# Two SwiGLU stages in seven block products each, with adaLN sums on VectorE, and x loaded first

## The reference

```python
def swiglu(h, w_gate, w_up, w_down):
    return (jax.nn.silu(h @ w_gate) * (h @ w_up)) @ w_down   # 1024 -> 2816 -> 1024
...
for l in range(DEPTH_2):                                     # two layers
    sh1, sc1, g1, sh2, sc2, g2 = jnp.split(c_act @ w_ada[l] + b_ada[l], N_MOD, axis=-1)
    ...
    x = layer_norm(DEEPNORM_ALPHA * x + g1[:, None, :] * y, ln1_g[l], ln1_b[l])
    h = modulate_2(x, sh2, sc2)
    y = swiglu(h, ffn_w_gate[l], ffn_w_up[l], ffn_w_down[l])
    x = layer_norm(DEEPNORM_ALPHA * x + g2[:, None, :] * y, ln2_g[l], ln2_b[l])
```

## Time and profile before

| | us |
|---|---|
| median of 3 runs | 1952.1 |
| lowest, highest | 1949.6, 1953.83 |
| profiled execution, its own time | 1950.68 |
| its span | 1948.9 |
| TensorE busy | 1888.5 |
| VectorE busy | 1291.9 |

### The profile page before, as it was taken

One profiled execution on the slowest core, in us unless ns is written; L12 is line 12 of the kernel. 1 busy time (PEld: TensorE's weight loads), 2 busy tenths in 40 slices (PEclk: granted clock), 3 DMA queues, 4 the chain that ended last, 5 costly groups with the idle time before them and its releaser, 6 DMA issues.

```text
span 1948.9 us, 23971 instructions
## 1 busy us (share of the span) xinstructions
PE 1888.5 (97%) x9600; PEld 1593.4 (82%) x9600; DVE 1291.9 (66%) x1969; ACT 814.6 (42%) x1238; POOL 466.0 (24%) x379
## 2 busy tenths in 40 slices
PE   4999999999999999999999999999999999999997
PEld 3788888887888887888788888877899778999996
DVE  6687655567667645665665555466677676777797
ACT  4677622352222235222522222248677553433333
POOL 4333210121111112001300000025643142445352
PEclk9999999999999999999999999999999999999998
DMA  9522366356565523542455442313211223323331
GB/s 334 153 85 66 113 222 238 120 193 238 211 221 201 188 87 117 186 151 93 168 201 187 173 151 87 108 65 130 71 58 52 87 72 101 109 95 101 108 100 52
DMA packets 134432, 267.65 MB, mean 137 GB/s; under 512 B 4576, under 2 KB 49648, under 8 KB 134321
## 3 DMA queue, kind: packets, MB, share of 16 engines
q1 hardware_dynamic: 129360, 248.59, 37.2%
q0 software_dynamic: 4960, 17.53, 2.5%
HBM read 261.84 MB, written 8.45 MB: 139 GB/s over the span
## 4 chain that ended last, share of the span: by engine, by line
PE 68%; DVE 3%; ACT 3%; POOL 2%; issue 1%; DVEq 0%; POOLq 0%; ACTq 0%
PE ps L720 22%; PE ps L722 21%; PE ps L721 21%; PE ps L880 1%; ACT t L1400 1%; ACT t L1396 1%; PE ps L869 1%; PE ps L858 0%; POOL t L2722 0%; PE ps L897 0%; PE ps L898 0%; PE ps L896 0%; DVE t L1889 0%; DVE t L1874 0%; POOL t L2531 0%
## 5 line engine op out<-in xcount | busy, mean ns | idle before, releaser
L720 PE MATMUL ps<-t 128*128 128x512 f32 (+1 forms) x2720 | 997.0, 367 | 12.1 <-POOL t L2626 5.2
L722 PE MATMUL ps<-t 128*128 128x512 f32 (+1 forms) x2720 | 989.6, 364 | 0.0
L721 PE MATMUL ps<-t 128*128 128x512 f32 (+1 forms) x2720 | 985.8, 362 | 0.0
L720 PEld LDWEIGHTS ps<-t 128*128 128x128 f32 x2720 | 513.2, 189 | 95.3 <-POOL t L2531 5.8
L722 PEld LDWEIGHTS ps<-t 128*128 128x128 f32 x2720 | 512.7, 189 | 84.6
L721 PEld LDWEIGHTS ps<-t 128*128 128x128 f32 x2720 | 513.1, 189 | 79.8 <-issue 1.0
L1810 DVE TENSOR_TENSOR t<-t 128x2048 fp32r<-128x2048 f32 x115 | 267.2, 2323 | 315.7 <-ACT t L1347 315.5
L1347 ACT ACTIVATE t<-t 128x2048 fp32r<-128x2048 f32 x115 | 219.7, 1911 | 465.2 <-PE ps L722 457.6
L1822 DVE CUSTOM_DVE_ANT_0 t<-t 128x1024 f32<-128x1024 f32 x144 | 174.8, 1255 | 6.8 <-DMA t<-in_adakv_t 3.6
L1874 DVE SCALAR_TENSOR_TENSOR t<-ps,t 128x512 f32<-128x512 f32 x184 | 131.7, 748 | 71.4 <-PE ps L722 68.1
L2531 POOL TENSOR_TENSOR t<-t 128x512 fp32r<-128x512 f32 x88 | 115.5, 1330 | 197.1 <-ACT t L1354 196.5
(11 more groups left out here) (196 smaller groups left out, 1894.7 us busy)
## 6 DMA issues: line engine op xcount, KB each, us to landing
t<-in_ada SPq DMA_DIRECT2D x48, 1024.0 KB, 5.9
t<-in_gate SPq DMA_DIRECT2D x22, 1024.0 KB, 5.2
t<-in_up SPq DMA_DIRECT2D x22, 1024.0 KB, 5.2
t<-in_down SPq DMA_DIRECT2D x22, 1024.0 KB, 5.1
t<-in_w_in SPq DMA_DIRECT2D x17, 1024.0 KB, 5.7
t<-in_w_mlp_in SPq DMA_DIRECT2D x16, 1024.0 KB, 5.3
t<-in_w_mlp_out SPq DMA_DIRECT2D x16, 1024.0 KB, 5.1
t<-in_ada_t POOLq DMA_DIRECT2D x13, 1024.0 KB, 6.2
```

The lines of the kernel that those rows point to most:

```text
L720: pe.matmul(o, wh, xh, start=first, stop=False)
L721: pe.matmul(o, wh, xl, start=False, stop=False)
L722: return pe.matmul(o, wl, xh, start=False, stop=last)
```

## The change

1. `plan_ffn2(l)` now plans both SwiGLU stages with S slots, in the order gate, up, gate, up instead of gate, gate, up, up (the last one had that), and `ffn2(l, ...)` is one function for both on each engine. The bank set of a slot is that of gate or up. One joined buffer each for gate and up remains (two before), and a spare one serves the second pair of weight sums (it was `csb[1]`, which the adaLN sums of the first SwiGLU read).
2. The 19 adaLN blocks of the first SwiGLU are spread over its slots 2 to 26 (counted from its first; 2, 3, 4, 6, 7, 8, 10, 11, 12, 14, 15, 16, 18, 19, 20, 22, 23, 24, 26), in two buffers instead of three. VectorE sums them at the end of the slot, behind the third join. SyncE loads each one slot ahead.
3. The second four shifts move from ahead of the joins of the first up slot of column group 5 to behind the third join of the last up slot; the column work `fox_cols` (before: `before()`, behind the residuals of the C slot) stands behind them in the first SwiGLU. Of group 5 the order is now gate, C slot of the down weights, up, gate, up (before: gate, C, gate, up, up).
4. Norm n4 modulates into eight tiles (`h_all[0]`, which the input sums read) instead of three buffers in turn.
5. At the start x is loaded ahead of the adaLN blocks 0 and 4; ScalarE squares x ahead of the bias rows and takes the root ahead of slot 0's pieces; VectorE adds the squares first, then sums block 0, makes the reciprocals and sums block 4; GpSimd takes low pieces and low tiles in turn; TensorE's units of slots 0 and 1 wait for the piece that they read.

The core of the diff:

```diff
+def plan_ffn2(l):
+    gate, up, down = (f"{w}{l}" for w in ("gate", "up", "down"))
+    for w, what in ((gate, "gate"), (up, "up")):
+        for p in range(2):
+            plan_role("A", w, 512 * p, 0, l, what, 0, p)
+    for f in range(4):
+        for p in range(2 if f else 0):
+            plan_role("S", gate, 0, 512 * f + 256 * p, l, "gate", f, p)
+            plan_role("S", up, 0, 512 * f + 256 * p, l, "up", f, p)
+        for hf in range(2):
+            plan_role("A", down, 512 * f, 512 * hf, l, "down", f, hf)
+    plan_role("S", gate, 0, 2560, l, "gate", 4, 0)
+    plan_role("S", up, 0, 2560, l, "up", 4, 0)
+    plan_role("S", gate, 0, 2048, l, "gate", 5, 0)
+    plan_role("C", down, 2560, 0, l, "down4", 4, 0)
+    plan_role("S", up, 0, 2048, l, "up", 5, 0)
+    plan_role("S", gate, 0, 2304, l, "gate", 5, 1)
+    plan_role("S", up, 0, 2304, l, "up", 5, 1)
+    for hf in range(2):
+        plan_role("A", down, 2048, 512 * hf, l, "down", 5, hf)
...
+ADA_FFN = stream_ada()
+for _j in range(ADA_FFN, len(ADA)):
+    _i = _j - ADA_FFN
+    _at = AT_FFN + 2 + _i * 24 // (len(ADA) - ADA_FFN - 1)
+    ADA_BUF[_j] = ("ffn", _i % 2)
+    ADA_LOADS.setdefault(_at - 1 if _i > 1 else AT_FFN, []).append(_j)
+    ADA_SUMS.setdefault(_at, []).append(_j)
...
             def job_unit(name, n, i, u, bank, site):
+                if n < 2:
+                    on.wait_ge(w_lo_p, "slot", n, u // 2)
+                elif u == 0:
+                    slot_lo(on, n)
                 if u == 0:
-                    slot_lo(on, n)
                     claim(bank)
...
                     if behind:
                         fourth(behind)
                     if raised:
                         times_gate(behind)
                     if in_products(n):
                         sums_lo(n, 1)
                     elif raised:
                         hidden_lo(behind)
                     if after and in_products(n + 1):
                         raw_lo(n + 1, 0)
                     if raised and in_products(n):
                         hidden_lo(behind)
                     slot[0] += 1
                     if after and in_products(n + 1):
                         raw_lo(n + 1, 1)
                     elif after and n + 1 not in PIECED:
                         convert(n + 1)
                     if (what, f, part) == ("gate", 5, 1):
                         shifts(0, 1, 2, 3)
-                    if (what, f, part) == ("up", 5, 0):
-                        shifts(4, 5, 6, 7)
...
                     if in_products(n):
                         first(n)
                     if after and in_products(n + 1):
                         sums_lo(n + 1, 0)
                     if in_products(n):
                         second(n)
                         third(n)
+                    sums_at(n)
+                    if (what, f, part) == ("up", 5, 1):
+                        shifts(4, 5, 6, 7)
+                        if before:
+                            before()
...
                 if BEFORE[n] is None:
-                    on.wait_ge(d_ada, "sum", len(ADA) - 1)
+                    on.wait_ge(d_evac, "up", l, 0, 3)
...
+            for k in range(1, KT):
+                add("n1", k)
             ada_sum(0)
+            roots("n1", False)
             ada_sum(4)
             two_columns(0)
-            for k in range(1, KT):
-                add("n1", k)
-            roots("n1", False)
...
-            for c in range(4):
+            for c in range(2):
                 piece(0, c)
-            for k in range(4):
+            for k in range(2):
+                low(k)
+            for c in (2, 3):
+                piece(0, c)
+            for k in (2, 3):
                 low(k)
...
             sp.dma_start(csb[0][:, :], a["c_b"]).then_inc(c_in[0].sem, c_in[0].up("landed", by=16))
-            ada_load(0)
-            ada_load(4)
             for hf in range(2):
                 k0 = 4 * hf
                 sp.dma_start(x_t[:, k0:k0 + 4, :], a["x_t"][k0 * P:(k0 + 4) * P, :].rearrange("(kt p) n -> p kt n", p=P)).then_inc(
                     x_in[hf].sem, x_in[hf].up("landed", by=16))
+            ada_load(0)
+            ada_load(4)
             load(0)
```

846 lines of the change are left out of this document (348 added, 498 removed).

## The result

The changed kernel takes 1962.88 us (median of 5 runs, 1961.8 to 1966.73), the kernel before 1952.84 beside it. The ratio is 1.0057, with a 95% interval of 1.0042 to 1.0072: slower by 0.57%, where 1939 us and "faster" were forecast. The profiled execution took 1961.8 us, its span is 1959.9. All executions of all kernels here lie within 0.3% of their kernel's median, but one in run e1 (2215.22 us at a mean granted clock of 0.79), which the ratios leave out.

What follows compares the result with a forecast made beforehand. TensorE, busy for 97% of the span, was taken as the bound. The terms - 18.0 + 10.0 + 2.5 + 1.0 - 8.5 = - 13.0 us gave 1939 us, range 1931 to 1948, or 1926 to 1955 with the rivals but for the outer ends.

Steps and rivals of the forecast that it cites:

- 18 S slots: First SwiGLU: eighteen slots take the seven-product form, each 1.00 us cheaper on TensorE, 18.0 us less.
- stalls of the three rounds: First SwiGLU: TensorE waits on a late VectorE queue, 3.3 us in rounds 1 and 3, 3.0 in round 2.
- C slot and tail, first SwiGLU: End of the first SwiGLU: 0.4 us stall for the C slot, 2.5 us for moved shifts and column work.
- last SwiGLU: Last SwiGLU's tail: the moved shifts make hidden values late, a wait of 1.2 us against 0.3 before, + 1.0.
- x first: Kernel start: loading x ahead of two adaLN blocks lets slot 2 begin at 53 to 54, 8.5 us sooner; bounds 3 and 10.
- The price of a block: First SwiGLU: an adaLN block takes 2.29 us of VectorE's queue; most GpSimd collision is only moved from the subtraction.
- the outcome at 0.12: Rival: VectorE becomes the first SwiGLU's bound, each block holding TensorE for its full length; 1954 or 1966 us, chance 0.12.
- The shifts: Both SwiGLU tails: shifts behind the last up slot's third join delay the down slot, + 2.5 (with column work) and + 1.0.
- Its own signs of being wrong: TensorE's first SwiGLU waits under 5 or over 20 us, slot 2 starting after 59, or that stage not faster than 366.

Runs made afterwards that it cites:

- e1: The kernel of a1 with the adaLN block of each up or gate slot ahead of the slot's first join instead of behind its last: 1952.29 us, ratio 0.9991.
- c1: The kernel of a1 with eight adaLN blocks left in the first SwiGLU, in down slots and slots 2 to 5, eleven summed in earlier stages: 1934.86 us, ratio 0.9906.
- a3: The changed kernel with GpSimd's four weight sums in the first SwiGLU made over 2 of every 128 columns: 1943.27 us, ratio 0.995.
- h3: The kernel of a1 with 14 adaLN blocks in the first SwiGLU, two, four and four in the rounds, none in the tail: 1942.82 us, ratio 0.9945.
- a1: The changed kernel with the four shifts back ahead of the joins and the column work back behind the copy slot: 1957.57 us, ratio 1.0021.
- a2: The changed kernel with the two instructions of each of the first SwiGLU's 19 adaLN blocks on 8 of 1024 columns: 1941.32 us, ratio 0.9943.
- b1: The kernel before with the new start alone (x first, part 5 of the change): 1947.07 us, ratio 0.9972.

## Why the prediction was wrong

| term | forecast | measured | from |
|---|---|---|---|
| 18 S slots | -18.0 | -17.5 | 366.10 - 348.63, the last SwiGLU before |
| stalls of the three rounds | +9.6 | +17.4 | windows after against 61.91 |
| C slot and tail, first SwiGLU | +2.9 | +10.4 | 106.72 - 96.31 |
| slots 0 to 3 and first down slots | 0 | +0.9 | 67.5 against 66.6 |
| last SwiGLU | +1.0 | +5.2 | 353.8 - 348.6 |
| x first, up to the first SwiGLU | -8.5 | -4.6 | 933.4 - 938.0 |
| between the SwiGLUs | 0 | -0.6 | 280.2 - 280.8 |
| sum | -13.0 | +11.2 | spans: +11.0 (the end behind the last SwiGLU is 0.2 shorter) |

**What held.** The S slots gain what the last SwiGLU promised; their groups of four took 39.94 us wherever VectorE was in time (c1, a3). TensorE waits where it was said to: on the pairs in the later S slots of each round, on the hidden values in round 2's down slot and at the end of the tail. That x could come first was right, and the last adaLN transfer didn't eat the gain.

**The step that failed** is the sum of the stalls, and in it what was put at nothing. The prediction counted two waits in the rounds, for the low halves of the pairs and of the hidden values, at 3.3 + 3.0 + 3.3 = 9.6 us. These two came to 6.7 + 3.1 = 9.8. The rounds lost 17.4. The other 7.6 us are terms that the sum doesn't have:
- The convert at each round's end, which waits on the chain fourth join, silu, ScalarE's convert: 1.0 us three times. The prediction said that "the A slots' converts, the loads and the number of weight sums stay".
- Taking up work again after a wait: 0.28 us each. In h3 a round's waits are 0.77 + 1.00 + 0.27 = 2.04, and the round is 2.88 us longer; the changed kernel has eleven such waits in its rounds, some 3 us.
- The half clock behind round 2's wait: 1.6 to 1.7 us. The prediction thought of the clock at the start only.

The tail of the first SwiGLU lost 10.4 us for 2.9. With the shifts back (a1) it still loses 6.6, where 0.4 stood for the C slot: waits of 1.13 at the copy slot, 1.84 on the pairs and 0.92 on the convert, and one of 2.44 at the norm, for 0.49 in the last SwiGLU.

**The price of a block** was wrong as well: "A block takes 2.29 us in the queue", and "most of that collision is only moved from the subtraction". It was not moved. In round 1 the blocks' instructions take 5.6 us more than in a3, while the subtraction of the pairs takes 10.23 us, hardly less than the 10.84 it takes in a round of the last SwiGLU. VectorE was busy for 60.3 to 60.8 us in a round, for 56.4 to 58.7 forecast. So it is luck in part that the two named waits still sum to what was forecast: another error, which no run singles out, made up for this one. It takes both things to make the loss: without GpSimd's sums the rounds lose 3.3 us of the 17.4 (a3), without the blocks' length nothing (a2). The prediction had the rule, had its trace row (2.30 against 1.23 us), and put the outcome at 0.12 because "the round still fits, 58.7 of 61.91 us". But 61.91 was the wrong line to hold it against. VectorE's queue has 4 to 6 us of idleness in a round that ScalarE and TensorE set. The runs put the line between three and four blocks; the change has five, four and five.

**The shifts** were the other mis-sized term: +2.5 and +1.0 forecast, with bounds of 4 each; 3.9 and 3.8 us by the stages of a1 (377.4 - 373.5, 353.8 - 350.0). The mechanism was right: the waits at the down slot behind them are 3.87 and 2.68 us, for the 1.2 worked out, and 2.5 with the column work. They are the shifts' own: in a2, where the adaLN sums take next to no time, they are 3.85 and 2.68 us. A half clock on top of each, 2.7 and 1.7 us, was not in the sum. By the medians of the runs the two cost 5.3 us and not 7.7; a1's profiled execution is 3.2 us below its median and the changed kernel's 1.1 below its own, which is 2.1 us of the difference. Among a1's ten executions the slower ones have the lower mean granted clock (0.989 to 0.990 in the six above 1957 us, 0.991 to 0.992 in the others).

**Its own signs of being wrong** came true in two of three: the first stage takes 377.4 us, more than 366, and TensorE's waits in it sum to 22.2, over 20. Slot 2 starts before 59.

**x first** was a matter of size: 5.7 us alone (b1) of the 8.5 forecast. The first product comes at 27.07 and not at 25, slot 2 at 56.15 and not at 53 to 54. The bounds, 3 to 10, hold it. The rest of the shortfall, 4.6 for 6.4 us, is mostly the half clock at 385.2 and 927.9.

**Left open:** e1's 5.3 us, which its profiled execution doesn't show; what decides whether a wait brings the half clock, on which several us of each time hang; and the norm behind the first SwiGLU, which begins 3.9 us after the stage's last plain product in every version with S slots there, after 2.6 in the kernel before. It wasn't tried on its own.

## What to carry to other kernels

An engine that is busy for 95% of a period is not 5% free when it works in order and waits for others in that period: find how much of its idleness is tied to another engine's event, and compare its work with what is left. Before giving VectorE two-input work in a stage in which GpSimd sums too, price each instruction at its length beside GpSimd (here 2.3 for 1.22 us) for as large a share as the stage's rows show, and look for slots in which GpSimd has none. Work that need not be done in the tight stage can go to a slack one: eleven blocks moved at a cost of 0.5 us at most, and the stage fell by 20. Before a difference between two stages is put down to their work, compare their granted clock.
